# Relative bias tile: stored 128 times and read back skewed, in place of a flip and one-hot products on TensorE

## The reference, cut to what matters

```python
def t5_bucket(dist):
    max_exact = NUM_BUCKETS // 2
    d = jnp.maximum(dist, 0)
    df = jnp.maximum(d, 1).astype(jnp.float32)
    large = max_exact + (jnp.log(df / max_exact) / math.log(MAX_DISTANCE / max_exact)
                         * (NUM_BUCKETS - max_exact)).astype(jnp.int32)
    large = jnp.minimum(large, NUM_BUCKETS - 1)
    return jnp.where(d < max_exact, d, large)
...
# compressed keys (15 of them, key n ends at position 16 n + 31)
s_c = einsum(qb, kc) * scale + head_bias[:, :, t5_bucket(t - cmp_end)];  p_c = masked_softmax(s_c, dist_c >= 0)
# selected and window keys
s_w = einsum(qb, kb) * scale + head_bias[:, :, t5_bucket(dist_w)];      p_w = masked_softmax(s_w, mask_w)
```

## Time and profile before

| | |
|---|---|
| median of 3 runs | 2390.87 us (2385.47 to 2393.47) |
| the profiled execution's own time | 2385.51 us |
| its span, first to last instruction | 2383.7 us |
| PE busy, share of the span | 2317.3 us, 97% |
| DVE busy | 1540.0 us, 65% |
| ACT busy | 1186.7 us, 50% |
| POOL busy | 61.8 us, 3% |
| mean granted TensorE clock | 0.983 |
| DMA, mean rate | 206 GB/s |

### The profile page before, as it was taken

How to read it: one execution, slowest core, us unless ns; L and a number is a source line. 1 busy time by engine, 2 the same in 40 slices (tenths; PEclk the granted TensorE clock), 3 DMA queues, 4 the chain that set the end, 5 groups by cost and what they waited for, 6 DMA issues and landing times.

```text
span 2383.7 us, 34430 instructions
## 1 busy us (share of the span) xinstructions
PE 2317.3 (97%) x15052; PEld 2084.3 (87%) x15052; DVE 1540.0 (65%) x1423; ACT 1186.7 (50%) x1158; POOL 61.8 (3%) x84
## 2 busy tenths in 40 slices
PE   8999999999999999999999999999999999799998
PEld 8997989799899889897998999788888998688886
DVE  4654656666466547456664566688887566588887
ACT  3333544443343346444333454477776454377774
POOL 1000100000000001000000000000000100000000
PEclk9999999999999999999999999999999899899999
DMA  6554434455555543435555455499997454499995
GB/s 222 181 194 154 132 126 152 158 169 185 187 177 178 194 160 126 160 126 172 182 185 183 142 181 190 142 330 344 369 348 281 145 180 156 143 336 347 344 370 190
DMA packets 309611, 490.91 MB, mean 206 GB/s; under 512 B 15348, under 2 KB 204964, under 8 KB 309456
## 3 DMA queue, kind: packets, MB, share of 16 engines
q1 hardware_dynamic: 305696, 475.35, 58.1%
q0 software_dynamic: 2912, 10.14, 1.2%
q10 hardware_dynamic: 848, 3.15, 0.4%
HBM read 487.53 MB, written 1.07 MB: 205 GB/s over the span
## 4 chain that ended last, share of the span: by engine, by line
PE 92%; DVE 5%; ACT 2%; issue 1%; POOL 0%; DMA 0%; DVEq 0%; ACTq 0%
PE PS L680 27%; PE PS L681 27%; PE PS L684 27%; PE PS L1321 1%; PE PS L895 1%; PE PS L860 1%; ACT RH L1432 1%; PE PS L834 1%; DVE RL L1916 1%; PE PS L845 1%; PE PS L1251 1%; DVE HTL L1902 1%; PE PS L1327 1%; DVE X L2252 1%; PE PS L1160 0%
## 5 line engine op out<-in xcount | busy, mean ns | idle before, releaser
L1916 DVE TENSOR_TENSOR RL<-RINGS,RH 128x2048 fp32r<-128x2048 f32 x448 | 1017.7, 2273 | 569.0 <-ACT RH L1432 566.2
L1432 ACT ACTIVATE RH<-RINGS 128x2048 fp32r<-128x2048 f32 x448 | 851.5, 1901 | 794.8 <-PE PS L684 794.5
L680 PE MATMUL PS<-RH,HTH 128*128 128x256 f32 (+3 forms) x1792 | 583.5, 336 | 6.6 <-DVE HTL L1898 3.9
L681 PE MATMUL PS<-RH,HTL 128*128 128x256 f32 (+3 forms) x1792 | 571.3, 330 | 0.0
L684 PE MATMUL PS<-RL,HTH 128*128 128x256 f32 (+3 forms) x1792 | 424.0, 327 | 0.0
L680 PE MATMUL PS<-HTH,RH 128*128 128x256 f32 x1536 | 408.5, 285 | 10.3 <-ACT RH L1432 5.0
L681 PE MATMUL PS<-HTL,RH 128*128 128x256 f32 x1536 | 405.0, 282 | 0.0
L680 PEld LDWEIGHTS PS<-RH,HTH 128*128 128x128 f32 x1792 | 346.6, 193 | 42.3 <-issue 8.1
L681 PEld LDWEIGHTS PS<-RH,HTL 128*128 128x128 f32 x1792 | 347.9, 194 | 28.8 <-issue 0.2
L684 PEld LDWEIGHTS PS<-RL,HTH 128*128 128x128 f32 x1792 | 311.5, 193 | 31.4
L684 PE MATMUL PS<-HTH,RL 128*128 128x256 f32 x1536 | 323.8, 282 | 1.5 <-DVE RL L1916 1.5
(11 more groups left out here) (411 smaller groups left out, 2268.1 us busy)
## 6 DMA issues: line engine op xcount, KB each, us to landing
RINGS<-w_in SPq DMA_DIRECT2D x64, 1024.0 KB, 5.0
RINGS<-w_gate SPq DMA_DIRECT2D x64, 1024.0 KB, 5.6
RINGS<-w_up SPq DMA_DIRECT2D x64, 1024.0 KB, 5.5
RINGS<-w_down SPq DMA_DIRECT2D x64, 1024.0 KB, 5.3
RINGS<-ffn_w_gate SPq DMA_DIRECT2D x44, 1024.0 KB, 5.2
RINGS<-ffn_w_up SPq DMA_DIRECT2D x44, 1024.0 KB, 5.2
RINGS<-ffn_w_down SPq DMA_DIRECT2D x44, 1024.0 KB, 4.8
RINGS<-w_out SPq DMA_DIRECT2D x16, 1024.0 KB, 4.8
```

The lines of the kernel that those rows point to most:

```text
L680: mm(dst, a_[0], b_[0], start=start, stop=False)
L681: mm(dst, a_[0], b_[1], start=False, stop=False) if left else mm(dst, a_[1], b_[0], start=False, stop=False)
L1432: A(splits.buffer(RH, RH3)[:, 0:width], RINGS[:, slot, 0:width], ACT.Copy).then_inc(wh_ready, 1)
L1916: TTn(RL[:, slot, 0:width], RINGS[:, slot, 0:width], splits.buffer(RH, RH3)[:, 0:width].bitcast(F32), ALU.subtract).then_inc(wl_ready, 1)
```

## The change

The DRAM scratch grows to 128 x 12 x 512. The store writes the 12 rows of VBIAS once for each of the 128 partitions, and the read takes from copy p the 256 values from 255 - p on, so the tile lands in BIAS in the right order and skewed. The flip on PE, its identity matrix, the one-hot matrix HOT with its load and its 60 products are gone. DVE adds the masks in place at the end of the pairs of the first feed-forward layer, in front of the splits of the down product, and at i = 2 of the attention stage copies the columns of the compressed keys out of BIAS; where no compressed key of the first query block is ever visible, the mask's values are copied.

```diff
-        BFLIP = TT[:, 0:12, :]
-        HOTR, HOT, VBIAS = (... for i, n in enumerate((32, 32, 12)))
+        HOTR, VBIAS = (... for i, n in enumerate((32, 12)))
@@ POOL
-            nc.gpsimd.dma_start(HOT, hot).then_inc(consts_loaded, 16)
...
                     pool.wait_ge(bias_row, 1)
-                    nc.gpsimd.dma_start(scratch, VBIAS).then_inc(bias_stored, 16)
+                    nc.gpsimd.dma_start(scratch.rearrange("r h n -> h r n"), spread(VBIAS, 1, P)).then_inc(bias_stored, 16)
                     pool.wait_ge(bias_stored, 16)
-                    nc.gpsimd.dma_start(BFLIP, bass.AP(tensor=scratch.tensor, offset=P, ap=[[1, P], [512, 12], [1, S]])).then_inc(bias_loaded, 16)
+                    nc.gpsimd.dma_start(BIAS, bass.AP(tensor=scratch.tensor, offset=S - 1, ap=[[12 * 512 - 1, P], [512, 12], [1, S]])).then_inc(bias_loaded, 16)
@@ PE, swiglu
-                    if l + f == 0 and j == 1:
-                        for t in range(T):
-                            for n in range(NCMP):
-                                u = t * P - 16 * n - 31 + 256
-                                last = mm(PS[:, 6, (t * NCMP + n) * 8:(t * NCMP + n + 1) * 8], HOT[:, u:u + P], RB[:, 0:8], start=True, stop=True)
-                        last.then_inc(hot_ready, 1)
                 if l + f == 0:
-                    pe.wait_ge(bias_taken, 4)
+                    pe.wait_ge(bias_row, 1)
@@ PE, attention
-                    if l == 0 and j == 0:
-                        pe.wait_ge(bias_loaded, 16)
-                        for b in range(6):
-                            last = mm(PS[:, 4 + b if b < 4 else b - 2, :], CON[:, O_FLIP:O_FLIP + P], BFLIP[:, 2 * b:2 * b + 2, :].rearrange("p h n -> p (h n)"), start=True, stop=True)
-                        last.then_inc(hot_ready, 1)
                     if j == 2:
-                        if l == 0:
-                            pe.wait_ge(bias_taken, 6)
@@ DVE, swiglu
-                    if l + f == 0 and j == 1:
-                        dve.wait_ge(hot_ready, 2)
-                        ... (four masked copies of 128 x 60 to BIASC)
+                if l + f == 0:
+                    dve.wait_ge(bias_loaded, 16)
+                    TTn(BIAS[:, 0:8, :], BIAS[:, 0:8, :], spread(CON[:, O_MB:O_MB + S], 1, 8), ALU.add).then_inc(bias_taken, 1)
+                    TTn(BIAS[:, 8:12, :], BIAS[:, 8:12, :], spread(CON[:, O_MS:O_MS + S], 1, 4), ALU.add).then_inc(bias_taken, 1)
@@ DVE, attention
-                    if l == 0 and i == 1:
-                        dve.wait_ge(hot_ready, 3)
-                        TTn(BIAS[:, 0:8, :], HIGH..., mask, ALU.add).then_inc(bias_taken, 1)
-                        TTn(BIAS[:, 8:12, :], LOW..., mask, ALU.add).then_inc(bias_taken, 1)
+                    if l == 0 and i == 2:
                         dve.wait_ge(zeroed, 4)
-                        dve.wait_ge(bias_taken, 6)
+                        dve.wait_ge(bias_taken, 2)
+                        for t in range(T):
+                            seen = 7 if t == 0 else NCMP
+                            first = P + 31 - t * P
+                            for r in range(2):
+                                own = BIASC[:, r * 8 + t * 4:r * 8 + t * 4 + 4, :]
+                                V.tensor_copy(own[:, :, 0:seen]..., BIAS[:, 0:8, first:first + 16 * seen - 15:16]...).then_inc(bias_taken, 1)
+                                if seen < NCMP:
+                                    V.tensor_copy(own[:, :, seen:NCMP], spread(CON[:, O_MCN + seen:O_MCN + NCMP], 1, 4)).then_inc(bias_taken, 1)
+                        dve.wait_ge(bias_taken, 8)
@@ host
-    scratch = nc.dram_tensor("bias_scratch", (12, 512), F32, kind="Internal").ap()
+    scratch = nc.dram_tensor("bias_scratch", (P, 12, 512), F32, kind="Internal").ap()
```

More of the change, by code:

```diff
@@ L65 @@
 VL = 52
[L67 to L71, removed]
+(O_ID, O_MB, O_MS, O_MC, O_MCN, O_SB, O_SBN, O_U, O_ONE, O_REV, O_CHO, O_NTH, O_FOLD) = (
+    0, 128, 384, 640, 670, 700, 1084, 1468, 1596, 1724, 1852, 1854, 1982)
+CONW = 1998
+NLOAD = 5
 UNITS = [(0, 0, 0, 4), (1, 0, 0, 4), (0, 1, 0, 2), (1, 1, 0, 2), (0, 1, 2, 2), (1, 1, 2, 2), (2, 0, 0, 2), (2, 1, 0, 2)]
@@ L206, in loop, with build @@
         c.after(m, count, per)
-def build(nc, a, out, con, hot_rev, hot, vect, scratch):
+def build(nc, a, out, con, hot_rev, vect, scratch):
     ctx = ExitStack()
@@ L290, in build @@
         BT = BTF.rearrange("p (a r n) -> p a r n", a=2, r=16)
-        BFLIP = TT[:, 0:12, :]
-        HOTR, HOT, VBIAS = (TT[0:n, 12 + 2 * i:14 + 2 * i, :].rearrange("p a n -> p (a n)") for i, n in enumerate((32, 32, 12)))
+        HOTR, VBIAS = (TT[0:n, 12 + 2 * i:14 + 2 * i, :].rearrange("p a n -> p (a n)") for i, n in enumerate((32, 12)))
         DIAG = TT[:, 18, :].rearrange("p (t n) -> p t n", t=T)
@@ L2085, in _ @@
                         outputs(i - 12)
-                    if l == 0 and i == 1:
-                        dve.wait_ge(hot_ready, 3)
-                        TTn(BIAS[:, 0:8, :], HIGH.rearrange("p (h n) -> p h n", h=8), spread(CON[:, O_MB:O_MB + S], 1, 8), ALU.add).then_inc(bias_taken, 1)
-                        TTn(BIAS[:, 8:12, :], LOW[:, 4 * S:8 * S].rearrange("p (h n) -> p h n", h=4), spread(CON[:, O_MS:O_MS + S], 1, 4), ALU.add).then_inc(bias_taken, 1)
+                    if l == 0 and i == 2:
                         dve.wait_ge(zeroed, 4)
-                        dve.wait_ge(bias_taken, 6)
+                        dve.wait_ge(bias_taken, 2)
[4 more added lines that the diff above has]
+                                own = BIASC[:, r * 8 + t * 4:r * 8 + t * 4 + 4, :]
+                                V.tensor_copy(own[:, :, 0:seen].rearrange("p (g i) n -> p g i n", g=2),
+                                              BIAS[:, 0:8, first:first + 16 * seen - 15:16].rearrange("p (g r i) n -> p r g i n", g=2, r=2)[:, r]).then_inc(bias_taken, 1)
+                                if seen < NCMP:
+                                    V.tensor_copy(own[:, :, seen:NCMP], spread(CON[:, O_MCN + seen:O_MCN + NCMP], 1, 4)).then_inc(bias_taken, 1)
+                        dve.wait_ge(bias_taken, 8)
                     if i == 3:
@@ L2643, in constants @@
     con[:, O_CHO:O_CHO + 2] = i // 64 == np.arange(2)[None, :]
-    con[:, O_FLIP:O_FLIP + P] = np.eye(P)[::-1]
     con[:, O_NTH:O_NTH + P] = 1 + np.arange(P)
@@ L2649, in constants @@
     hot_rev = (t5_bucket(383 - w) == b).astype(np.float32)
-    hot = (t5_bucket(w - 256) == b).astype(np.float32)
-    return con, hot_rev, hot
+    return con, hot_rev
 def input_order():
@@ L2690 @@
     arrays = {n: np.ascontiguousarray(x) for n, x in inputs.items()}
-    for n, x in zip(("con", "hot_rev", "hot"), constants()):
+    for n, x in zip(("con", "hot_rev"), constants()):
         arrays[n] = x
@@ L2696 @@
     out = nc.dram_tensor("out", (1, S, D), F32, kind="ExternalOutput").ap()
-    scratch = nc.dram_tensor("bias_scratch", (12, 512), F32, kind="Internal").ap()
-    build(nc, aps, out, aps["con"], aps["hot_rev"], aps["hot"], aps["vect"], scratch)
+    scratch = nc.dram_tensor("bias_scratch", (P, 12, 512), F32, kind="Internal").ap()
+    build(nc, aps, out, aps["con"], aps["hot_rev"], aps["vect"], scratch)
     r = run(nc, [arrays], core_ids=[0])
```

## The result

The change made the kernel slower: 2409.14 us median (2408.76 to 2410.54, 4 runs) against 2389.59 us (2385.47 to 2393.47, 4 runs) of the kernel before, ratio 1.0077, 95% interval [1.0063, 1.0092]. The forecast was 2376.5 us in a range of 2369 to 2406; the time lies 33 us above the one and 3 us above the other. The profiled execution of after took 2409.12 us, with a span of 2407.3 us. That of before was the fastest of its runs, so the two traces differ by 23.6 us where the medians differ by 19.6.

What follows compares the result with a forecast made beforehand. The prediction took PE, busy 97% of the span, as the bound. Its terms, -10.10 - 5.14 + 0 + 0 + 0.9 = -14.3 us, took the 2390.87 us median to 2376.6 (point 2376.5), range 2369 to 2406.

Steps and rivals of the forecast that it cites:

- The two terms of PE: First feed-forward layer: dropping 60 compressed-key products saves 10.10 us; attention stage: dropping the flip saves 5.14 us.
- The masks on DVE: Two additions behind the last pair's second split take 3.51 us, hidden by DVE's idle time and lead: cost 0.
- the small copies: Six copies at i = 2 of the attention stage, 0.9 us together: cost 0, at worst 0.9 us.
- DVE's new wait: Before the down product's splits, at 156.9 us, DVE waits for the read; everything landed 87 us ahead.
- The turn-taking of DMA engines: Store beside weight loads: engines alternate packets, 0.235 us a turn, so a load of 64 takes about 15 us.
- term 5: Store of 3.15 MB beside early weight loads: 11.8 us plus loss to the loads, costing PE about 0.9 us.
- Rival A: Store beside early weight loads: neighbouring rows read slowly, PE idles 25.7 us, net +12.1, median 2403; chance 0.38 with tail.

Runs made afterwards that it cites:

- the DRAM copies: Changed kernel, but VBIAS stored once and its 128 copies made by one DRAM-to-DRAM transfer: 2382.67 us, ratio 0.9971.
- The pieces: Changed kernel with its 3 MB store from 12 neighbouring partitions cut into 8 parts, one every two chunks: 2383.34 us, ratio 0.9972.
- one copy: Changed kernel with the store of 24 KB made once and the read at the old stride, biases in wrong order: 2380.08 us, ratio 0.9964.
- rows spread: Changed kernel with the 12 stored rows in partitions 0, 4, ... 44, same bytes and destination: 2394.77 us, ratio 1.0015.
- the two with the old program: The kernel before, 2389.59 us, and the kernel before with only an unused 3 MB store added, 2404.67 us, ratio 1.0062.
- the five with padding: Useless products added per feed-forward layer: DRAM copies with 9, 0.9921; with 5, 0.9937; with 9 and eight pieces, 0.9921; changed kernel, 9, 1.0042; kernel before, 9, 0.9998.

## Why the prediction was wrong

**What held.** The two terms of PE: 10.10 and 5.14 us foreseen, and the rhythm of the chunks shows both gone, with the clock at its higher level where it had fallen. The masks on DVE and the small copies cost nothing. DVE's new wait was never late. The turn-taking of DMA engines, packet by packet, held too: it is the mechanism of the stall. That the load took 15 us beside the DRAM copies, as foreseen beside the store, is luck as a number: 15 was 64 turns of 0.235 us, and there each engine had eight packets of about 1.06 us.

**The step that failed** is the duration of the store in term 5: "I take 11.8 us plus what it loses to the weight loads." It was 45.1 us to landing, 0.60 us a packet. The prediction had both values, 0.185 and 0.62, and took the wrong one, on the ground that the small store's packets took about 0.1 us each. Those were twelve packets in one microsecond; a row of a short burst was read as a rate. The long store itself began with quick packets too, and came to the slow pace 0.8 us after its start. Rival A gave the mechanism, the packet (0.62 us), the landing of the load (80.5; it was 82.5, and 64 turns of 0.62 + 0.049 us from 39.5 on give 82.3) and the stall with its clock (27.3 us; it was 28.2), and had 0.38 of the chance. That the pace depends on which partitions are read was shown by moving the rows four apart. The Trainium skill, "SBUF — State Buffer", "Door 1: The DMA port swizzle", lets groups of four neighbours share one port of 27.2 GB/s. The long store agrees: four packets of 4 KB in 0.60 us are 27 GB/s for a group. The pieces don't: the second moved its 0.39 MB in 3.0 us, 131 GB/s where three ports would give 82. Why a burst is faster no run here shows. I had that sentence and gave it too little weight.

**A term that was missing.** Even rival A's 2403 was 6 us short. PE's program became 144 instructions shorter, and the gather products, 1300 us later, then waited 15.7 us in four for "issue" where it had been 8.1 in two. The five kernels with the shorter program (the change, one copy, rows spread, DRAM copies, the store in pieces) have 13.5 to 15.7 us in four; the two with the old program and the five with padding have 7.8 to 8.5 in two. This follows the PE program and neither the stall nor the time of the stage. The traces show that these are waits for packets of instructions. The longer wait in the first expert layer is one between two gather products, which the other programs don't have; why it comes with one place of the products in the program and not with another is not shown. By ratios it costs (1.0077 - 1.0042) x 2390 = 8 us in the changed kernel. Between the DRAM copies with and without padding it is 8 of the 12 us, by the two traces with the same clock. With the padding the change stands at +10 us, against +12 of rival A.

**The range** ended at 2406, rival A's centre and a little more. It left no room for A with anything added.

## What to carry to other kernels

A long DMA that reads few neighbouring partitions can be slow (0.60 us for 4 KB here, against 0.26 with the rows four apart). Since the engines take turns packet by packet, it slows the loads beside it to its own pace for as long as it lasts (41.75 us here for a load that takes 5.2). A large one should come from DRAM or in short bursts; rows spread apart helped by half (PE waited 7.5 us instead of 26.7). A single short transfer is no measure of a rate. When instructions leave an engine's program, look at the waits for "issue" of that engine at far places too, before the difference is put down to the change itself.

## What was not expected of the hardware

The place of code mattered by about 8 us of 2390: PE waited 5.3 us for instructions in the middle of 32 like products, and the granted clock fell to its lower level behind it, both gone with 20 useless products elsewhere. And copying from DRAM to DRAM, 3 MB in 14.7 us beside the weight loads, was three times as fast as storing the same bytes from twelve neighbouring partitions, 45.1 us. The best version, copies from DRAM to DRAM with padding, takes 2370.65 us, 0.8% less than the kernel before.
